# Three k-tile pairs of eight in the seven-product form, with the order of an FFN's first product rewritten

## What is computed

```python
def swiglu(x, w_gate, w_up, w_down):
    return (jax.nn.silu(x @ w_gate) * (x @ w_up)) @ w_down

h = x
h = h + 0.5 * swiglu(rms_norm(h, ffn1_norm), ffn1_w_gate, ffn1_w_up, ffn1_w_down)
u = rms_norm(h, mix_norm)
...  # attention, gated linear attention, merge gates, branches, out projection
h = h + merged @ w_out
h = h + 0.5 * swiglu(rms_norm(h, ffn2_norm), ffn2_w_gate, ffn2_w_up, ffn2_w_down)
h = h + sigmoid(rms_norm(h, ple_norm) @ w_ple_gate) * (p @ w_ple_proj)
return rms_norm(h, final_norm)
```

## Time and profile before

| what | value |
|---|---|
| median of 3 runs | 2248.66 us (2248.65 to 2249.57) |
| profiled execution, device time | 2249.12 us |
| its span | 2247.1 us |
| TensorE busy | 2217.0 us, 99% |
| VectorE busy | 1337.5 us, 60% |
| ScalarE busy | 1050.7 us, 47% |

### The profile page before, as it was taken

How to read it: one execution, slowest core, us unless ns; L and a number is a source line. 1 busy time by engine, 2 the same in 40 slices (tenths; PEclk the granted TensorE clock), 3 DMA queues, 4 the chain that set the end, 5 groups by cost and what they waited for, 6 DMA issues and landing times.

```text
span 2247.1 us, 24310 instructions
## 1 busy us (share of the span) xinstructions
PE 2217.0 (99%) x9950; PEld 1827.4 (81%) x9950; DVE 1337.5 (60%) x1318; ACT 1050.7 (47%) x1147; POOL 40.4 (2%) x71
## 2 busy tenths in 40 slices
PE   8999999999999999999999998899999999999998
PEld 7888888888888888877778887788878888888886
DVE  5777544677555444445655654777754467755555
ACT  6445434454444444464444443454543345544454
POOL 0000000000010000010000000000000000000000
PEclk9999999999999999999999999999999999999999
DMA  8455456555465666665655664555546664556654
GB/s 312 177 202 205 164 196 205 207 186 191 175 201 187 198 195 190 175 179 173 174 168 159 187 187 143 213 172 203 207 149 191 204 221 171 197 178 212 187 189 147
DMA packets 161079, 425.66 MB, mean 189 GB/s; under 512 B 11320, under 2 KB 11328, under 8 KB 143568
## 3 DMA queue, kind: packets, MB, share of 16 engines
q1 hardware_dynamic: 159216, 419.21, 57.3%
q0 software_dynamic: 1472, 4.70, 0.8%
q10 hardware_dynamic: 288, 0.30, 0.0%
HBM read 422.06 MB, written 2.11 MB: 189 GB/s over the span
## 4 chain that ended last, share of the span: by engine, by line
PE 97%; DMA 1%; DVE 1%; ACT 0%; issue 0%; ACTq 0%; POOLq 0%; POOL 0%
PE acc L1470 18%; PE acc L1472 18%; PE acc L1471 18%; PE acc L1513 6%; PE acc L1515 6%; PE acc L1514 6%; PE turn L1515 4%; PE turn L1513 4%; PE turn L1514 4%; PE fox L1515 4%; PE fox L1514 4%; PE fox L1513 4%; DMA raw<-in_ffn_up 1%; PE turn L1490 1%; PE acc L1507 0%; PE turn L1762 0%
## 5 line engine op out<-in xcount | busy, mean ns | idle before, releaser
L1003 DVE TENSOR_TENSOR w_lo<-raw,w_hi 128x1024 fp32r<-128x1024 f32 x451 | 557.9, 1240 | 604.0 <-ACT w_hi L573 603.6
L573 ACT ACTIVATE w_hi<-raw 128x1024 fp32r<-128x1024 f32 x451 | 477.0, 1060 | 704.0 <-PE acc L1472 633.9
L1470 PE MATMUL acc<-w_hi,x_both 128*128 128x512 f32 x940 | 370.7, 394 | 2.8 <-DVE x_both L1165 2.8
L1472 PE MATMUL acc<-w_hi,x_both 128*128 128x512 f32 x940 | 366.3, 390 | 0.0
L1471 PE MATMUL acc<-w_lo,x_both 128*128 128x512 f32 x940 | 365.9, 389 | 0.0
L1470 PE MATMUL acc<-w_hi,slab_r 128*128 128x512 f32 x832 | 325.9, 392 | 2.6 <-DVE w_lo L1003 2.6
L1472 PE MATMUL acc<-w_hi,slab_r 128*128 128x512 f32 x832 | 324.5, 390 | 0.0
L1471 PE MATMUL acc<-w_lo,slab_r 128*128 128x512 f32 x832 | 324.4, 390 | 0.0
L1058 DVE TENSOR_TENSOR w_lo<-raw,w_hi 128x2048 fp32r<-128x2048 f32 x84 | 192.2, 2290 | 100.8 <-ACT w_hi L629 100.3
L629 ACT ACTIVATE w_hi<-raw 128x2048 fp32r<-128x2048 f32 x84 | 161.2, 1919 | 191.1 <-PE fox L1515 93.5
L1470 PEld LDWEIGHTS acc<-w_hi,x_both 128*128 128x128 f32 x940 | 176.5, 188 | 44.8 <-issue 5.7
(11 more groups left out here) (368 smaller groups left out, 3200.9 us busy)
## 6 DMA issues: line engine op xcount, KB each, us to landing
raw<-in_ffn_up SPq DMA_DIRECT2D x88, 1024.0 KB, 4.9
raw<-in_ffn_w_down SPq DMA_DIRECT2D x176, 512.0 KB
raw<-in_w_in SPq DMA_DIRECT2D x96, 512.0 KB
more<-in_ffn_up SPq DMA_DIRECT2D x46, 1024.0 KB, 4.9
raw<-in_w_merge_gate SPq DMA_DIRECT2D x64, 512.0 KB
raw<-in_ffn_up SPq DMA_DIRECT2D x37, 512.0 KB, 4.0
raw<-in_w_out SPq DMA_DIRECT2D x32, 512.0 KB
raw<-in_w_ple_gate SPq DMA_DIRECT2D x32, 512.0 KB
```

What stands on the lines that cost most here:

```text
L573: nc.scalar.activation(w_hi[:, slot, :, :], raw[:, slot, :, :], ACT.Copy).then_inc(hi_split, 1)
L1003: nc.vector.tensor_tensor(w_lo[:, slot, :, :], raw[:, slot, :, :], w_hi[:, slot, :, :].bitcast(F32), ALU.subtract).then_inc(lo_split, 1)
L1470: nc.tensor.matmul(to, hi(kt)[:, tok], w_hi[:, slot, k, :], start=kt == 0, stop=False)
L1472: last = nc.tensor.matmul(to, lo(kt)[:, tok], w_hi[:, slot, k, :], start=False, stop=kt == BK * nb - 1)
```

## The change

Three units of eight (US = 3) are done in the seven-product form. A stage with neighbours on both sides is now B0 S3 B1 S4 A0 B2 S5 A1 S6 A2 S7, and a phase's first stage S0 S1 S2 S3 A0 S4 S5 A1 S6 A2 S7. The third unit's two kept tiles lie in `corner`, which the attention's masks also use; its formed tile lies in a spare tile of `more`. So its B item is split in two instructions on each of ScalarE and VectorE. GpSimd writes the masks later, once the first FFN's last use of `corner` is over. `copy_parts` and `combine` move from the end of a stage to behind the split of the next stage's first item. The activation sums have one buffer for the raw sums instead of two, so each unit goes VectorE, ScalarE, VectorE before the next, and stand at k=2 instead of k=1 and k=3. In up2a, SP waits for the end of `out` ahead of the third load only.

```diff
@@ stage_of: the order of one pair's items
-US = 2
+US = 3
     own = [("S", pair, u) for u in range(UNITS)]
     if pair > first:
-        own = [("B", pair, 0), own[US], ("B", pair, 1), *own[US + 1:]]
+        b0, b1, b2 = [("B", pair, u) for u in range(US)]
+        own = [b0, own[US], b1, own[US + 1], b2, *own[US + 2:]]
     if pair + 1 < pairs:
-        later = [("A", pair + 1, u) for u in range(US)]
-        own = [*own[:-2], *later, *own[-2:]]
+        a0, a1, a2 = [("A", pair + 1, u) for u in range(US)]
+        own = [*own[:4], a0, *own[4:6], a1, own[6], a2, own[7]]
@@ memory
-        room, room_r = shared(("room", [P, 9, COLS], F32), ("room_r", [P, 9, COLS], F32R))
+        room, room_r = shared(("room", [P, 11, COLS], F32), ("room_r", [P, 11, COLS], F32R))
+        corner = sb("corner", [P, 2 * COLS])
...
+        def later_tiles(name, u):
+            if u < 2:
+                return (trio(name, u),)
+            return corner.rearrange("p (a c) -> p a c", a=2), more(name)[0][:, 15:16, :]
@@ SyncE, the loads of an FFN's first product
-                if up == "up2a":
-                    sp.wait_ge(multiplied, BLOCK[up])
                 for stage in STAGES[up]:
                     for it in stage:
+                        if up == "up2a" and it.at == BLOCK[up] + 2:
+                            sp.wait_ge(multiplied, BLOCK[up])
...
                             sp.wait_ge(lo_split, it.trio_free)
-                            sp.dma_start(trio(up, it.unit)[:, 0:2, :], source[:, 2:4, :])
+                            sp.dma_start(later_tiles(up, it.unit)[0][:, 0:2, :], source[:, 2:4, :])
@@ GpSimd
             nc.gpsimd.memset(minus_half[:], -0.5).then_inc(ident_ready, 1)
+            root(0)
+            pool.wait_ge(multiplied, BLOCK["down1b"])
             nc.gpsimd.memset(ones[:], 1.0).then_inc(pool_chain, 1)
...
-            root(0)
-            pool.wait_ge(multiplied, BLOCK["down1b"])
@@ ScalarE, split_item (VectorE's has the same loop)
-                nc.scalar.activation(hi_quad(name, it.quad)[:, 0:n, :], of[:, 0:n, :], ACT.Copy)\
-                    .then_inc(hi_split, item_counts(name, it))
+                at = 0
+                for of in later_tiles(name, it.unit) if it.kind == "B" else (raw_quad(name, it.raw),):
+                    n = of.shape[1]
+                    last = nc.scalar.activation(hi_quad(name, it.quad)[:, at:at + n, :], of, ACT.Copy)
+                    at += n
+                last.then_inc(hi_split, item_counts(name, it))
@@ ScalarE, up_phase
                         split_item(name, it)
+                        if k == 0 and n > 0:
+                            copy_parts(name, pair)
...
-                        if k == 3 and n == 0 and sums is not None:
+                        if k == 2 and n == 0 and sums is not None:
                             split_sums(sums)
...
-                    if pair + 1 < pairs:
-                        copy_parts(name, pair + 1)
@@ VectorE, make_sums and up_groups
-            def make_sums(name, hi, lo, sums):
+            def make_sums(hi, lo, first):
                 for u in range(US):
...
                     nc.vector.tensor_tensor(to[:, 3, :], a12, to[:, 1, :], ALU.subtract).then_inc(sums_made, 1)
-                    dve.wait_ge(sums_made, sums + u + 1)
...
                     dve.wait_ge(sums_hi, first + u + 1)
+                    nc.vector.tensor_tensor(s_lo[:, u, :, :], to, s_hi[:, u, :, :].bitcast(F32), ALU.subtract)\
+                        .then_inc(sums_lo, 1)
+                    dve.wait_ge(sums_lo, first + u + 1)
...
+                        if k == 0 and n > 0:
+                            combine(name, pair)
...
-                            if sums is not None:
-                                make_sums(name, hi, lo, sums)
-                        if k == 3 and n == 0 and sums is not None:
-                            split_sums(sums)
+                        if k == 2 and n == 0 and sums is not None:
+                            make_sums(hi, lo, sums)
...
-                    if pair + 1 < pairs:
-                        combine(name, pair + 1)
```

More of the change, by code:

```diff
@@ L214, in build @@
         ident = sb("ident", [P, P])
[L215 to L218, removed]
+        causal, up_to = corner[:, 0:3 * P], corner[:, 3 * P:4 * P]
+        later_in_chunk, ones, thin_rows = corner[:, 4 * P:5 * P], corner[:, 5 * P:6 * P], corner[:, 6 * P:8 * P]
         in_chunk = sb("in_chunk", [P, 2])
@@ L262, in trio @@
         def trio(name, u):
[L263 to L270, removed]
+            return more(name)[0][:, 12:15, :] if u == 0 else room[:, 8:11, :]
+        def later_tiles(name, u):
+            if u < 2:
+                return (trio(name, u),)
+            return corner.rearrange("p (a c) -> p a c", a=2), more(name)[0][:, 15:16, :]
+        s_hi = room_r[:, 0:3, :].rearrange("p u (s c) -> p u s c", s=4)
+        s_lo = room_r[:, 3:6, :].rearrange("p u (s c) -> p u s c", s=4)
+        m1_copy, m5_copy = room[:, 6, :], room[:, 7, :]
         x_t = slab[:, SLABS - KD:, :, :].rearrange("p k t c -> p k (t c)")
@@ L402, in feed_forward @@
                             sp.wait_ge(lo_split, it.trio_free)
-                            sp.dma_start(trio(up, it.unit)[:, 0:2, :], source[:, 2:4, :]).then_inc(trio_full[it.unit], 16)
+                            sp.dma_start(later_tiles(up, it.unit)[0][:, 0:2, :], source[:, 2:4, :]).then_inc(trio_full[it.unit], 16)
                 b = BLOCK[down]
@@ L620, in split_item @@
             def split_item(name, it):
-                n = 3 if it.kind == "B" else 4
-                of = trio(name, it.unit) if it.kind == "B" else raw_quad(name, it.raw)
                 if it.kind == "S":
@@ L1053, in split_item @@
             def split_item(name, it):
-                n = 3 if it.kind == "B" else 4
-                of = trio(name, it.unit) if it.kind == "B" else raw_quad(name, it.raw)
                 dve.wait_ge(hi_split, it.at + 1)
-                nc.vector.tensor_tensor(lo_quad(name, it.quad)[:, 0:n, :], of[:, 0:n, :],
-                                        hi_quad(name, it.quad)[:, 0:n, :].bitcast(F32), ALU.subtract)\
-                    .then_inc(lo_split, item_counts(name, it))
+                at = 0
+                for of in later_tiles(name, it.unit) if it.kind == "B" else (raw_quad(name, it.raw),):
+                    n = of.shape[1]
+                    last = nc.vector.tensor_tensor(lo_quad(name, it.quad)[:, at:at + n, :], of,
+                                                   hi_quad(name, it.quad)[:, at:at + n, :].bitcast(F32), ALU.subtract)
+                    at += n
+                last.then_inc(lo_split, item_counts(name, it))
             def make_steps(name, it):
@@ L1065, in make_steps @@
                 dve.wait_ge(trio_full[it.unit], 16 * it.trio_count)
-                q, b = raw_quad(name, it.raw), trio(name, it.unit)
+                q, later = raw_quad(name, it.raw), later_tiles(name, it.unit)
+                w21, w22 = later[0][:, 0, :], later[0][:, 1, :]
+                t4 = later[0][:, 2, :] if len(later) == 1 else later[1][:, 0, :]
                 after_own(nc.vector.tensor_tensor(q[:, 1, :], q[:, 2, :], q[:, 0, :], ALU.subtract))
-                nc.vector.tensor_tensor(q[:, 2, :], b[:, 1, :], q[:, 2, :], ALU.subtract)
-                after_own(nc.vector.tensor_tensor(q[:, 3, :], b[:, 1, :], q[:, 1, :], ALU.subtract))
-                nc.vector.tensor_tensor(b[:, 2, :], b[:, 0, :], q[:, 3, :], ALU.subtract).then_inc(steps_made, 1)
+                nc.vector.tensor_tensor(q[:, 2, :], w22, q[:, 2, :], ALU.subtract)
+                after_own(nc.vector.tensor_tensor(q[:, 3, :], w22, q[:, 1, :], ALU.subtract))
+                nc.vector.tensor_tensor(t4, w21, q[:, 3, :], ALU.subtract).then_inc(steps_made, 1)
             def combine(name, pair):
```

27 lines of the change are left out of this document (10 added, 17 removed).

## The result

The changed kernel takes 2272.22 us (median of four runs, 2269.09 to 2274.31) against 2249.11 us (2248.65 to 2250.51) for the kernel before on the same chip: a ratio of 1.0101, 95% interval 1.0083 to 1.0118. It is slower, as predicted: the medians part by 23.1 us, where the sum had 14.4. The profiled execution of after is its fastest, 2269.09 us with a span of 2266.9; against the span of before that is +19.8 us.

A forecast was written before the change was run, and what follows sets the result against it. TensorE's matmul queue, busy 99% of the span, was taken as the bound. -11.56 + 23.3 + 4.95 + 0.8 - 3.05 = +14.4 on 2249.12 gave 2263.5, forecast as 2263 us; range 2250 to 2276.

The forecast's parts named there:

- the walk through the middle of a stage: Stages with B and A items: A2's loads wait for S5's split and hold up S6; TensorE waits 1.79 us.
- A2's loads are in time: Rival, middle of a stage: S6's split ready 1.8 us sooner, the 23.3 us go, 2239 us; chance 0.15.
- the second rival: Loads issued close together slow A2's pair: 2272 us if it suffers by 0.7 us, 2281 by 1.35; chance 0.12.
- The wait in each stage: 13 x 1.79 = 23.3: In 13 stages with both B and A items, TensorE waits 1.79 us for S6's split: +23.3 us.
- Loads delay each other: Rival, A2's pair of loads: slower by 0.7 us gives 2.5 a stage, 2272 us; by 1.35, 2281; chance 0.12.
- The clock in up1a's wait: Rival: the clock falls in up1a's 4.95 us wait too, fourth item about 3.0 us slower, 2265 us; chance 0.2.
- The sums, up1a: Up1a's first stage: three units of sums ahead of the fourth item's split make TensorE wait, +4.95 us.
- S6 of that stage: Up1a's first stage: S6 ready at 98.5 against TensorE's 97.7, +0.8 us.
- Up2a and SP's wait: Start of up2a: earlier loads remove waits and a slow first item, the sums give most back: -3.05 us.
- Copies and additions: Moved behind the next stage's first split, done with 1.2 us to spare: 0; without cover, 1.7 us per 0.1 over.
- Masks: Written by GpSimd in down1b, ten short instructions used two phases later: 0.
- -11.56: Fewer matmuls on TensorE: 3 saved in each of 17 pairs, 51 x 0.2267 us, -11.56 us.

The follow-up runs named there:

- the fastest kernel: The changed kernel with A2's steps behind S6's split and the activation sums spread over the first stage: 2221.06 us, ratio 0.9878 to the kernel before.

## Why the prediction was right, and where its sizes were off

**The sign and the mechanism.** The step that decided was the walk through the middle of a stage. Its links came out as 4.8 for a landing of 4.75, 2.67 for steps of 2.66, and 1.81 for 1.79; both experiments on it, one that moves the steps and one that shrinks the loads, remove just those waits. The rival "A2's loads are in time" did not happen. The sizes were less good: 2272.22 lies in the range, but above the 2256 to 2270 of the forecast itself, and it is near the second rival's 2272 without having come by that rival's path. Some misses also cancelled: the clock cost 4.8 us more than forecast, and 5.6 us at down2a and at the start went the other way.

**The wait in each stage: 13 x 1.79 = 23.3 was too small by about 4 us**, by two terms:
- The landing of 4.75 held in the first FFN: 4.6 to 4.8 us in its six stages, and 1.65, 1.62 and 1.71 us of idle time in up1a. In the second FFN it was 4.6 to 5.4, with 5.4 for the loads issued at 1498.13 and 1589.23, whose waits are the two of 2.4. The 13 idle times sum to 23.4 us. That is the mild end of "Loads delay each other"; which loads did it was not tried.
- A wait costs more than its idle time. The idle time is counted from the modelled end of the last matmul, 0.16 us behind the due start (1.81 - 1.65), and the first matmul behind a wait takes 0.33 us to the next start (142.97 to 143.30), not 0.2267. So each wait costs its idle time and about 0.27. The chain gave 1.79 to the due start and so had the first part, but not the second. 23.4 + 13 x 0.27 = 26.9.

**The clock.** The prediction let it fall behind the wait of 9 us only, and it did so there: the item from 1437.63 took 8.45 us, for 8.48 before. The rival "The clock in up1a's wait" (0.2) was what happened: behind the 4.67 us, 10 matmuls' starts span 3.68 us (74.66 to 78.34), 1.6 more than at full clock. TensorE: Matmul & The Clock Gate, Why this matters for your kernels, in the Trainium skill, which advises against idle gaps in mid-kernel, would have been the better forecast here than the earlier trace rows. The stretch of the earlier trace rows, 1423 to 1426, lies inside the wait of 2.98 us and not behind it; behind it the clock was at 1.00 too, as the row above shows. And the clock fell where no rival had it, behind 2.39 us at 1508.59 and 2.36 us at 1599.74, 1.6 us each by the same count. Together +4.8 us. The step that failed was to take one row, 1.00 behind 2.98 us, for a rule.

**The sums, up1a** (+4.95): 4.67 idle and 0.27, 4.94. S6 of that stage (+0.8): 0.24 idle, 0.5 in all.

**Up2a and SP's wait** (-3.05): no wait between `out` and up2a, and a new one of 8.96 at 1437.63, as forecast. Smaller waits at 1487.42 (0.61) and in up2b's first stage at 1864.02 (0.65) were not in the sum. The prediction had said of up2b's that S6 is ready 1.6 us ahead there; it was so in neither. In up1b it was ready only 0.1 us ahead (its split ends at 449.20, TensorE starts it at 449.31): A1's steps start 6.3 us behind the issue of A1's second load (427.77 to 434.03), and the split of S5, which A2's loads wait for, stands behind them. In up2b these were 6.6 us, and A2's steps started 5.2 us behind the issue of its second load, for 4.8 in up1b; that is the wait.

**What the prediction had not looked at.** The wait of 2.56 us at the start of down2a, with its slow matmuls, is in before as well, and the change removes it: 2.7 us in up2a's row of the table (the wait ends at down2a's first matmul) and 1.7 in down2a's. It goes with the number of items in up2a, as the rows of ScalarE above show. The start of the kernel, 1.2 us shorter in this execution, differs as much between executions of kernels that are alike there (10.57 to 12.41 us to the first matmul of the w_in blocks).

**The terms at zero.** Copies and additions: no wait at B0, S0 or A2 in after's list, as forecast. But "0" was against the kernel before; in the fastest kernel they cost 10 us without the move, and the prediction gave only a price for it and not this size. In the changed kernel itself the move was not undone. Masks: the phases around down1b are unchanged.

**The sum anew**, on the spans: -11.56, + 26.9 stage waits, + 4.94 and 0.5 in up1a, - 9.5 in front of up2a, + 9.1 + 3.0 for the fourth item there, less 3.25 and 3.04 for the third item's wait and the slow first item of before, + 1.8 for two small waits, + 4.8 clock, - 4.4 around down2a, - 1.2 start: +18.1 of +19.8. The last 1.7 us I don't place.

## What to carry to other kernels

Where a queue is in order, put work that waits for a late transfer behind the work that doesn't, even if its own consumer then has less slack: four short instructions a stage, moved by one place, were worth some 32 us, three times what the change saved in matmuls. Work done once per phase is as dangerous as work done each time if it stands in one piece in front of a full-rate consumer. When waits are counted, add a restart to each and, for those of 2 us and more, the chance of a slow clock, and look for the waits that are already in the kernel.

## What the hardware showed that I had not expected

- Between 2 and 3 us, whether the clock fell behind a wait can't be told from the wait's length. It stood at 1.00 behind 2.98 us in before, and at 0.53 behind the same 2.98 us in before with SP's narrowed wait; at 0.62 behind 2.96 and at 1.00 behind 2.93 us in one execution. It fell even behind 1.99 us once (with SP's wait as it was), and in the same execution it stayed at 1.00 behind 2.21 us, 1618.10 to 1621.50:

```profile
1571.49 0.50 PE L1514 MATMUL acc<-w_hi,y_r 128*128 128x512 f32 x1 [1.99 <-DVE w_lo L1063]
...
1571.50:1575.00 3.50, 3.50 (x10) 2.75 (x11) 3.50 (x2) 1.49 (x1) 0.00 (x0) 0.66 0.72 239
```

  Behind all waits of 4.67 us and more it fell. A kernel with many waits of this kind also spreads more: 5.2 us over four runs of after and 5.7 over ten of the kernel with the sums spread alone, against 1.7 over the four of late steps and spread sums. That the clock is what makes the spread was not tried.
- The second of two 512 KB loads has no one landing time. In after, A2's landed 4.7 us behind its issue at 133.16 in up1a and 5.4 at 1498.13 in up2a, with the same three issues of SyncE in a row (1497.71, 1498.13 and 1500.24 there, 132.74, 133.16 and 135.45 in up1a). Over the 13 stages it is 4.6 to 5.4.
